# Two-layer hybrid attention and expert kernel: level exponents by whole heads, top levels as blocks, two masked matrices, and a second product that begins with the last group

## What is computed

```python
def step(S, inp):                      # hgrn2, one chunk
    qc, kc, lfc, vc = inp
    b = jnp.cumsum(lfc, axis=2)
    o_inter = jnp.einsum('bhtk,bhkv->bhtv', qc * jnp.exp(b), S)
    diff = b[:, :, :, None, :] - b[:, :, None, :, :]
    decay = jnp.exp(jnp.where(causal[:, :, None], diff, MASK_VALUE))
    A = jnp.einsum('bhtk,bhsk,bhtsk->bhts', qc, kc, decay)
    o_intra = jnp.einsum('bhts,bhsv->bhtv', A, vc)
    ...
    return S_new, o_inter + o_intra

def block(xb):                         # peer_ffn
    ...
    top_s, pos = lax.top_k(cand_s, PEER_TOPK)
    idx = jnp.take_along_axis(cand_i, pos, axis=-1)
    gate = jax.nn.softmax(top_s, axis=-1)
    act = jax.nn.gelu(jnp.einsum('thkd,td->thk', u[idx], xb).astype(jnp.float32), approximate=False)
    return jnp.einsum('thk,thkd->td', (gate * act).astype(xb.dtype), v[idx])

def reference(x, p, ...):
    ...
    for i in range(DEPTH):
        mix = hybrid_mixer(h, w_in[i], ...)
        h = layer_norm(DEEPNORM_ALPHA * h + mix, ln1_g[i], ln1_b[i])
        ffn = peer_ffn(h, peer_wq[i], peer_keys[i], peer_u[i], peer_v[i])
        ple = jax.nn.sigmoid(h @ ple_gate_w[i]) * (p[i] @ ple_w[i])
        h = layer_norm(DEEPNORM_ALPHA * h + ffn + ple, ln2_g[i], ln2_b[i])
    return h
```

## Time and profile before

| | us |
|---|---|
| timed runs, median of 3 (lowest to highest) | 3617.3 (3616.1 to 3617.6) |
| profiled execution, its own time | 3620.2 |
| span of the profiled execution | 3618.3 |
| PE, DVE, POOL, ACT busy | 3359.6, 2799.6, 2097.9, 1149.4 |
| mean granted clock of PE | 0.97 |

### The profile page before, as it was taken

How to read it: one execution, slowest core, us unless ns; L and a number is a source line. 1 busy time by engine, 2 the same in 40 slices (tenths; PEclk the granted TensorE clock), 3 DMA queues, 4 the chain that set the end, 5 groups by cost and what they waited for, 6 DMA issues and landing times. The chain is left out here.

```text
span 3618.3 us, 48025 instructions
## 1 busy us (share of the span) xinstructions
PE 3359.6 (93%) x17690; PEld 2977.9 (82%) x17690; DVE 2799.6 (77%) x5751; ACT 1149.4 (32%) x1902; POOL 2097.9 (58%) x1388
## 2 busy tenths in 40 slices
PE   6998799999989999999889977999999998999996
PEld 5787687999989978888777866879998997888885
DVE  5966339998986489999967843599989764899998
ACT  1234012343433333333222430123433333333332
POOL 5910575776656655555478025767765666555553
PEclk9999899999999999999989988999999999999998
DMA  3300222888778899999722002248887789999994
GB/s 127 94 24 19 70 88 104 284 285 302 276 249 295 325 372 354 354 355 355 247 82 93 1 30 82 82 168 266 297 300 246 278 306 343 343 354 355 352 357 175
DMA packets 316648, 822.03 MB, mean 227 GB/s; under 512 B 22400, under 2 KB 122752, under 8 KB 313088
## 3 DMA queue, kind: packets, MB, share of 16 engines
q1 hardware_dynamic: 112256, 349.15, 28.3%
q0 software_dynamic: 73728, 268.47, 20.1%
q10 hardware_dynamic: 130432, 201.34, 15.9%
HBM read 716.12 MB, written 102.76 MB: 226 GB/s over the span
## 5 line engine op out<-in xcount | busy, mean ns | idle before, releaser
L1158 POOL TENSOR_TENSOR u_lo<-panel,u_hi 128x1024 fp32r<-128x1024 f32 x256 | 616.9, 2410 | 269.4 <-ACT u_hi L991 267.6
L555 PE MATMUL ps<-hT_hi,u_lo 128*128 128x384 f32 x2048 | 707.3, 345 | 6.2 <-POOL u_lo L1158 6.2
L555 PE MATMUL ps<-hT_lo,u_hi 128*128 128x384 f32 x2048 | 689.1, 336 | 0.0
L555 PE MATMUL ps<-hT_hi,u_hi 128*128 128x384 f32 x2048 | 688.7, 336 | 0.0
L555 PE MATMUL ps<-v_hi,w_lo 128*128 128x512 f32 x1536 | 600.3, 391 | 28.9 <-DVE w_lo L1660 28.9
L1111 POOL TENSOR_TENSOR ring_hi<-panel,cst 128x512 fp32r<-128x512 f32 x244 | 270.6, 1109 | 570.7 <-PE ps L538 332.4
L555 PE MATMUL ps<-v_hi,w_hi 128*128 128x512 f32 x1536 | 599.9, 391 | 0.0
L555 PE MATMUL ps<-v_lo,w_hi 128*128 128x512 f32 x1536 | 599.8, 391 | 0.0
L1175 POOL TENSOR_TENSOR v_lo<-panel,v_hi 128x1024 fp32r<-128x1024 f32 x128 | 348.5, 2723 | 396.3 <-ACT v_hi L1027 388.0
L991 ACT CAST u_hi<-panel 128x1024 fp32r<-128x1024 f32 x256 | 268.1, 1048 | 727.5 <-PE ps L555 710.9
L1027 ACT CAST v_hi<-panel 128x1024 fp32r<-128x1024 f32 x256 | 269.5, 1053 | 678.3 <-PE ps L555 678.3
(11 more groups left out here) (232 smaller groups left out, 6030.5 us busy)
## 6 DMA issues: line engine op xcount, KB each, us to landing
panel<-in_u SPq DMA_DIRECT2D x256, 512.0 KB, 4.4
panel<-in_v SPq DMA_DIRECT2D x256, 512.0 KB, 6.9
act_scratch<-arena ACTq DMA_DIRECT2D x128, 384.0 KB, 4.4
gate_scratch<-arena ACTq DMA_DIRECT2D x24, 2048.0 KB, 9.4
arena<-act_scratch ACTq DMA_DIRECT2D x64, 768.0 KB, 6.9
arena<-gate_scratch ACTq DMA_DIRECT2D x64, 768.0 KB, 14.3
panel<-in_w_in SPq DMA_DIRECT2D x28, 1024.0 KB, 5.2
panel<-in_wq SPq DMA_DIRECT2D x16, 1024.0 KB, 5.2
```

Source lines behind the costliest of these rows:

```text
L555: mm = nc.tensor.matmul(o, lhs[a], rhs[b_], start=(start and n == 0), stop=(stop and n == 2))
L1158: pr.mark(nc.gpsimd.tensor_tensor(u_lo[:, j % URING].rearrange("p c n -> p (c n)"), u_tile(j), u_hi[:, j % URING].rearrange("p c n -> p (c ...
```

## The change

**Levels.** The buffers now hold a whole head: 7 levels of 128x512, in two places (even heads in `lng`, `pTs` and 512 columns of the arena, odd heads in `rows_mem`). Exponents are written in two parts, levels 1 to 4 at the first step of the head before, 5 to 7 at the second; the exponential follows at the end of the second step in three instructions; keys and queries are multiplied in at the third and fourth. `level_products` has six 128x128 products (levels 0 to 5) in one go. Levels 6 and 7 are made as three block products (two of 32x32, one of 64x64) that write over the upper part of level 0's result; level 0's mask lets them through. `masked` copies six 128x128 results into two matrices: one multiplication each for the first, then predicated copies, each after the first two waiting for the last but one. `hg_outputs` multiplies two matrices instead of eight.

```diff
-                    for k in range(4):
-                        lev = 4 * half + k
-                        kk = kT[:, hd, toks] if lev == 0 else zed(j)[:, lev - 1, :]
-                        qq = hqT[:, hd, toks] if lev == 0 else zed(j)[:, lev - 1, :]
-                        mm = nc.tensor.matmul(level_bank(half)[:, k * P:(k + 1) * P], kk, qq, start=True, stop=True)
+                    for lev in range(MASKED):
+                        kk, qq = (level(lev), level(lev)) if lev else (kT[:, hd, toks], hqT[:, hd, toks])
+                        mm = nc.tensor.matmul(level_bank(lev // 3)[:, lev % 3 * P:(lev % 3 + 1) * P], kk, qq,
+                                              start=True, stop=True)
+                        if lev == 0:
+                            for top_, s0, n in ((6, 0, 32), (6, 64, 32), (7, 0, 64)):
+                                nc.tensor.matmul(level_bank(0)[s0:s0 + n, s0 + n:s0 + 2 * n],
+                                                 level(top_)[:, s0:s0 + n], level(top_)[:, s0 + n:s0 + 2 * n],
+                                                 start=True, stop=True)
...
-                    for lev in range(LEVELS):
-                        mm = nc.tensor.matmul(hg_o_bank[:, 0:HD], AT[:, j % 2, lev, :], vv,
-                                              start=(lev == 0 and i == 0), stop=(lev == LEVELS - 1))
+                    for g in range(2):
+                        mm = nc.tensor.matmul(hg_o_bank[:, 0:HD], AT[:, j % 2, g, :], vv,
+                                              start=(g == 0 and i == 0), stop=(g == 1))
...
-                    if j + 3 < NH:
-                        level_exps(j + 3)
+                    if j % NT == 1 and j // NT + 1 < HH:
+                        level_exps(j // NT + 1)
...
+                    dve.wait_ge(a_done.sem, layer * a_done.per_layer + j + 1)
+                    for k in range(3):
+                        for g in range(2):
...
+                            if k == 0:
+                                pr.mark(nc.vector.tensor_tensor(at, got, where, ALU.mult), at_ready)
+                            else:
+                                dve.wait_ge(at_ready.sem, layer * at_ready.per_layer + MASKED * j + 2 * k + g - 1)
+                                pr.mark(nc.vector.copy_predicated(at, where.bitcast(U32), got), at_ready)
...
-                        if j + 3 < NH:
-                            exponents(j + 3)
+                        ahead, turn_ = j // NT + 1, j % NT
+                        if ahead < HH and turn_ < 2:
+                            exponents(ahead, (LOW, HIGH)[turn_])
                         fox_sum(2 * j)
-                        if j + 2 < NH:
-                            times_keys_queries(j + 2)
+                        if ahead < HH and turn_ >= 2:
+                            times_keys_queries(ahead, (LOW, HIGH)[turn_ - 2])
```

```diff
+LATE_DOTS = 6
+ADDED = [0] * (LATE_DOTS + 1)
+for tile_ in range(LATE_DOTS + 1, NK):
+    ADDED.append(ADDED[-1] + 1 + (tile_ % 4 == 0 and ADDED[-1] < tile_ - 3))
...
-                    if j == 2 * TILE_SLOTS:
+                    if j == 6 * TILE_SLOTS:
                         sp.wait_ge(dotted.sem, layer * dotted.per_layer + SLOTS)
...
-                pe.wait_ge(gelu_done.sem, layer * gelu_done.per_layer + NK)
...
+                        if j == 0 and k in ABANKS:
+                            pe.wait_ge(gelu_done.sem, layer * gelu_done.per_layer
+                                       + max(u for u in range(NK) if ABANKS[u % 3] == k) + 1)
...
+                        pr.mark(nc.scalar.copy(gin(0)[:, b_], gmat[:, b_ % 2, NK - GROUP:NK, :]), last_gates)
...
-                weights(0)
                 low_v(0)
+                weights_first(0)
+                weights_first(1)
+                low_w(0)
+                weights_first(2)
+                low_w(1)
                 low_v(2)
-                pr.mark(nc.vector.tensor_copy(acc0, h[:, 0, :]), acc0_ready)
-                low_w(0)
-                low_w(1)
+                weights_first(3)
                 for j in range(NK):
-                    if j % GROUP == 0 and j // GROUP + 1 < UPANELS:
-                        weights(j // GROUP + 1)
                     if j + 2 < NK:
                         low_w(j + 2)
                     if j + URING < NK:
                         low_v(j + URING)
+                    if j % GROUP == 1 and j // GROUP + 1 < UPANELS:
+                        weights(j // GROUP + 1)
+                    if j < LATE_DOTS:
+                        dot(SLOTS - LATE_DOTS + j)
```

More of the change, by code:

```diff
@@ L40 @@
 LEVELS = 8
+MASKED = 6
 STAIR = [TOPK // (a + 1) for a in range(TOPK)]
@@ L347, in build @@
         u_lo_ready = sig("u_lo_ready", NK)
-        act_out = [sig(f"act_out{r}", 16 * UPANELS) for r in range(2)]
+        act_out = [sig(f"act_out{r}", 16 * (UPANELS - 1)) for r in range(2)]
         hot_ready = sig("hot_ready", NG)
@@ L865, in _, with level_exps @@
                 pr.mark(last, d_exp)
-                def level_exps(j):
-                    act.wait_ge(lev_ready.sem, layer * lev_ready.per_layer + j + 1)
-                    pr.mark(nc.scalar.activation(zed(j), zed(j), ACT.Exp), lev_exp)
-                for j in range(3):
-                    level_exps(j)
+                def level_exps(hd):
+                    act.wait_ge(lev_ready.sem, layer * lev_ready.per_layer + hd + 1)
+                    for piece in zed_pieces(hd):
+                        last = nc.scalar.activation(piece, piece, ACT.Exp)
+                    pr.mark(last, lev_exp)
+                level_exps(0)
                 act.wait_ge(hdec_ready.sem, layer * hdec_ready.per_layer + 1)
@@ L1165, in _ @@
                         gather_u(j - 3)
-                for s in range(NK - 3, SLOTS):
+                for s in range(NK - 3, SLOTS - 1):
                     gather_u(s)
-                pool.wait_ge(a_full.sem, layer * a_full.per_layer + NK)
                 def v_lo_part(j):
@@ L1178, in _ @@
                 v_lo_part(1)
+                gather_u(SLOTS - 1)
+                v_lo_part(3)
+                pool.wait_ge(a_full.sem, layer * a_full.per_layer + NK)
                 for s in range(3):
                     gather_v(s)
-                for j in range(NK):
+                sent = 3
+                for j in range(1, NK):
                     if j + URING < NK:
                         v_lo_part(j + URING)
-                    if j + 3 < SLOTS:
-                        gather_v(j + 3)
+                    while sent < min(j + 4, SLOTS, VBUF + (ADDED[j - 2] if j > 1 else 0)):
+                        gather_v(sent)
+                        sent += 1
+                for s in range(sent, SLOTS):
+                    gather_v(s)
         @block.vector
@@ L1330, in _, with exponents @@
                 pr.mark(nc.vector.tensor_tensor(kd, kd, kT, ALU.mult), hdec_ready)
-                def exponents(j):
-                    hd, i = j // NT, j % NT
-                    toks = slice(i * P, (i + 1) * P)
-                    if j >= ZRING:
-                        dve.wait_ge(a_done.sem, layer * a_done.per_layer + 2 * (j - ZRING) + 2)
-                    for lev in range(1, LEVELS):
+                def exponents(hd, levels):
+                    if hd >= 2:
+                        dve.wait_ge(a_done.sem, layer * a_done.per_layer + NT * (hd - 1))
+                    for lev in levels:
```

191 lines of the change are left out of this document (106 added, 85 removed).

## The result

The changed kernel takes **3573.1 us** (median of 4 runs, 3567.2 to 3580.5), the kernel before 3616.7 (4 runs). The ratio is 0.9882, 95% interval 0.9862 to 0.9903: 1.2% faster. The forecast was 3556 with a range of 3535 to 3585. The sign and the range held; the gain is 43.6 us where 61 were expected.

The account below looks back on a forecast made before the run. PE, busy 93% of the span, was taken to bound the kernel. From the profiled 3620.2 us, 35 (head loops) and 25.7 (second product's start) come off: 3559.5, or 3556 against the median; range 3535 to 3585.

Parts of the forecast that it names:

- Removed, 1.79 us per step for eight products: Head loop: two of eight level products and six of eight value products leave PE, 1.79 us per step.
- Small products, 0.5 us, about 0.17 each: Head loop: the three block products add 0.5 us per step to PE, between ends of 0.22 and 1.23.
- DVE and ACT: Head loop: DVE's 128x256 multiplications take 0.42 us, DVE gets lighter; ACT's exponentials take some 3.7 us per head.
- Changes of head, 6 us: Head loop: late exponentials and z cost PE 1 us per change of head, 6 us in all, bounds 0 and 12.
- Head loops, 35 us less: Both head loops: 41.3 us saved on PE minus 6 at changes of head, 35 less (10 to 50).
- Stall of 3.2 us at tile 4: Second product, first fetched group: gates land 14.1 us after issue; PE stalls 3.2 us plus 1.9 for the clock, per layer.
- second rival: Both good ends: small products near 0.25 us and no stall at tile 4; time about 3540, chance 0.17.
- fetch(2): Second product's start: its issue may hold ACT's queue 6.05 us; w_hi(3) at T + 11.5, needed T + 12.2, just hidden.
- second term: Start of the second product: 35.9 us lost before, minus 10.2 for stalls at tile 4, so 25.7 us less.
- third rival: Second product: landing stays 20 us, gain 12 instead of 26, time 3570; second stall at tile 8, 3580; chance 0.13.
- the 35.9: Start of the second product: loss in the kernel before, 20.7 us in layer 1 and 15.2 in layer 0.
- The body costs nothing: Body of the second product: weights moves to a group's second tile; DVE has 8% to spare, cost put at 0.

Follow-up runs that it names:

- second: Kernel before with only the second product's part of the change, head loop as before: 3600.3 us, ratio 0.9958 (8 runs).
- twice: Changed kernel with every block product of levels 6 and 7 done two times: 3594.0 us (one run).
- after_again: The changed kernel once more, unaltered: 3571.1 us, ratio 0.9879 to the kernel before.
- late_rows: Changed kernel with the gathers of v's rows put off, none before tile 5, then two more each tile: 3561.5 us, ratio 0.9852.

## Why the prediction was right or wrong

The forecast was 17 us too low; the sign and the range held. By its own steps:

- **PE bounds both stretches**: right. DVE lost 114 us of work and ACT's long exponentials came, and the time followed PE's.
- **Removed, 1.79 us per step for eight products**: right. Without any block product a loop is 24.6 us shorter than before, and PE waits 3.6 us in it at changes of head (half of 4.5 and 2.7 us in both layers together), where it waited 0.6 before: 27.6/16 = 1.73.
- **Small products, 0.5 us, about 0.17 each**: near in the sum, wrong in the parts. In the loops they cost 0.51 to 0.58, in the rows of a step 0.64: a 32x32 0.09, the 64x64 0.26, and 0.19 for the way in and out, a term that the sum didn't have. The rule of the Trainium skill that I weighed, load time in proportion to columns ("TensorE: Matmul & The Clock Gate", section LDWEIGHTS), would have put them near 0.22 together: not so here, even the blocks by themselves take 0.44. That the step gains by blocks at all, which the change took for granted, is false: two whole products take 0.44, twice the 0.22 that I had read from the rows.
- **DVE and ACT**: right. 128x256 took 0.42 us (419 ns, as estimated), the exponentials of a head 1.91 + 1.47 = 3.4 us (3.7 estimated).
- **Changes of head, 6 us**: right, 5.0 measured, against 1.3 of such short waits in the loops of before; but more than half, 2.7, is PE's wait for DVE's last products of z and not for ACT.
- **Head loops, 35 us less**: 32.9 with the clock at full, 28.0 in the profiled execution, 26 on the mean of the drops seen. A step is 7.47 us (from 2014.37 to 2044.25 for four), and I had said 7.0 to 7.4. The failed step is one that wasn't in the sum: I took it that PE's clock in the loop stays at full, because the trace of before showed 1.00 there. The shape of the work decides that too, and the change altered it.
- **No gap between the products, full clock there**: right.
- **Stall of 3.2 us at tile 4**: wrong for the changed kernel's two executions. The gates of fetch(1) landed in 10.1 us in layer 0 and 8.1 in layer 1; from 0.5 to 9.3 us after T no packet of a gather moved. I had this in the second rival and took 14.1. But the margin is thin. Of the 14 starts of a second product in the traces that leave the gathers as they are, two have the stop at tile 4, 3.8 us (`second`, layer 0) and 1.5 (`twice`, layer 0), and these two have none at tile 8.
- **fetch(2)**: the failed step of the second term. I checked its issue, which holds ACT's queue, and not its landing. Its issue was no harm; in `after_again` that of fetch(3) was, 2.1 us ahead of tile 5. The landing took 30.5 and 32.0 us, because POOL's gathers of v start about 5 us after the issue and take their share of the DMA engines. The stops of 4.4 and 5.5 us with the slow clock behind them (2.4 and 2.6 us) are 15 us; I had 10.2 for another tile. The third rival named the place, tile 8, and priced a stall there at 10 us (it was 15), but gave the wrong reason (that fetch(2) is queued behind fetch(1)); `late_rows` shows that it is the gathers. Measured for the whole term, from the end of the first product as I had reckoned: 18.2 us in the profiled pair and 16.1 in `second`, instead of 25.7. Taking the stops from the 35.9 would leave 20.9; of the 2.7 us between, 1.1 are more clock lost behind layer 0's second product (6.6 us against 5.5), and the rest stays open. With the gathers put off it is 30.3 (11.9 and 18.4), above the forecast and below the 35.9 of no stall at all.
- **The body costs nothing**: right, save for waits for `w_lo` of 0.7 to 3.2 us some 90 to 106 us after the first product's end, which all later traces but `after_again` have in one layer or both. The first trace has none.
- **The sum**: 7.5 us are missing at the second product, 2.1 in the loops at full clock and 5.0 by the three drops, 14.6 together of the 17. The remaining 2.5 have no row: the profiled execution is the fastest of its four, 6 us below their median, and gains 6.2 in the middle stretches, which no term of the forecast had. That the forecast lies 17 off and not 8, as in the profiled pair, is a matter of executions.

## What to carry to other kernels

Before you cut a product into blocks, price the blocks by their shape, and the way in and out of them: here a 64x64 fp32 block took 0.26 us, a whole 128x128 product 0.22, and going in and out 0.19, so masking whole products on an engine with room to spare was the better trade. When a wait goes, ask what starts at the moment that it freed, on every queue: for the transfer that is needed next, count the bytes that others put beside it, and hold back those that nobody needs yet. A range should also have a term for PE's clock wherever the change alters the mix of products.

## What the runs showed of the hardware

PE's granted clock was 0.50, the level of 1.2 GHz, for 3.4 us at a time in a loop in which PE stood still for 2.5 us of 124 and never for more than 1.2 at once: 1.9 times per loop with small products, 0.2 times without them. "TensorE: Matmul & The Clock Gate" of the Trainium skill (section HAM oscillation — how this bites in real kernels) ties such falls to gaps of PE; here PE was busy 10.00 of the 10 us ahead of the first, so the traces don't bear that out for these.

A whole 128x128 fp32 product next to smaller ones took 0.1 us longer on either side of them (0.37 against 0.28 ahead, 1.00 against 0.89 for the four behind).

The landing time of the same 768 KB was 8.1 us while no gather took part (3006 to 3014 us: ACT's queue 71% of the engines, 345 GB/s in all) and 32.0 with eight gathers issued meanwhile (35%, 387 GB/s).
